# Ten modulation rows moved from the two first-block mixers to GpSimd, which makes them during the feed-forwards

## The reference, cut to what matters

```python
mod = cond @ w_ada[l] + b_ada[l]                 # cond = silu(c), one vector of 1024; w_ada[l] is 1024 x 9216
sh1, sc1, g1, sh2, sc2, g2, sh3, sc3, g3 = split(mod, 9)
y = swiglu(modulate(x, sh1, sc1), ...)           # feed-forward, inner width 2816
x = post_norm(x, y, g1, 0.5, ...)
y = token_mixer(modulate(x, sh2, sc2), w_in, w_out)
x = post_norm(x, y, g2, 1.0, ...)
y = swiglu(modulate(x, sh3, sc3), ...)           # second feed-forward
x = post_norm(x, y, g3, 0.5, ...)
```

## Time and profile before

| what | value |
|---|---|
| median of 3 runs | 2607.93 us (2603.06 to 2611.44) |
| profiled execution, device time | 2608.47 us |
| its span from first to last instruction | 2606.7 us |
| mean granted TensorE clock | 0.879 of full speed |
| busy: PE, PEld, DVE, ACT, POOL | 2114.2, 1335.6, 1023.4, 526.1, 71.9 us |
| feed-forward 1 of layer 1 | 44 to 236 us |
| first mixer | 251 to 452 us |
| feed-forward 2 of layer 1 | 464 to 656 us |
| feed-forward 1 of layer 2 | 674 to 866 us |
| second mixer | 882 to 1080 us |
| feed-forward 2 of layer 2 | 1092 to 1285 us |
| second block | 1285 us to the end |

### The profile page before, as it was taken

The page is one execution under the profiler, slowest core; times in us unless marked ns, Lnnn a source line. Parts: engine busy times, 40 slices in busy tenths (PEclk is TensorE's granted clock), DMA queues, the critical chain, the costliest instruction groups (busy, mean ns, idle before and its releaser), DMA issues.

```text
span 2606.7 us, 34365 instructions
## 1 busy us (share of the span) xinstructions
PE 2114.2 (81%) x12932; PEld 1335.6 (51%) x12932; DVE 1023.4 (39%) x1644; ACT 526.1 (20%) x858; POOL 71.9 (3%) x106
## 2 busy tenths in 40 slices
PE   6998987999899897799979676666659877777775
PEld 4996454899799545599865421211128542221111
DVE  3886134778887404588723300000022331000002
ACT  2332031443343103233312200000010110000000
POOL 1000000000000000000100000000000000000000
PEclk7998988999899898899989788888879978777777
DMA  9986742888588565488740699999995469999996
GB/s 335 321 306 218 277 139 105 301 302 304 204 297 299 191 253 194 154 301 296 274 147 18 255 405 410 410 410 410 410 389 187 164 246 410 409 410 410 409 409 247
DMA packets 289374, 758.09 MB, mean 291 GB/s; under 512 B 17616, under 2 KB 125424, under 8 KB 289184
## 3 DMA queue, kind: packets, MB, share of 16 engines
q1 hardware_dynamic: 282368, 737.34, 75.4%
q0 software_dynamic: 6688, 19.78, 2.3%
q10 hardware_dynamic: 256, 0.13, 0.0%
HBM read 756.01 MB, written 1.18 MB: 290 GB/s over the span
## 4 chain that ended last, share of the span: by engine, by line
PE 61%; DMA 24%; DVE 5%; SPq 4%; ACT 2%; issue 2%; DVEq 1%; ACTq 0%
PE psum L693 20%; DMA W<-in_w_exp_down 14%; PE psum L705 9%; DMA W<-in_w_exp_up 8%; PE psum L756 6%; PE psum L733 4%; SPq L485 4%; PE psum L1063 3%; PE psum L1039 3%; PE psum L1002 3%; PE psum L635 1%; PE psum L1027 1%; PE psum L904 1%; DMA W_mod<-in_mod_w 1%; PE psum L666 1%
## 5 line engine op out<-in xcount | busy, mean ns | idle before, releaser
L693 PE MATMUL psum<-parts 128*128 128x256 f32 x4224 | 528.8, 286 | 14.7 <-DVE parts L1490 7.4
L693 PEld LDWEIGHTS psum<-parts 128*128 128x128 f32 x4224 | 526.2, 195 | 22.4 <-issue 16.2
L1002 PE MATMUL psum<-W,scr 128*32 128x512 f32 x2048 | 316.5, 729 | 141.0 <-DMA W<-in_w_exp_up 125.9
L705 PE MATMUL psum<-parts 128*128 128x512 f32 x1056 | 257.8, 393 | 0.0
L1002 PEld LDWEIGHTS psum<-W,scr 128*32 128x32 f32 x2048 | 54.1, 118 | 378.7 <-DMA W<-in_w_exp_up 284.3
L1854 DVE TENSOR_TENSOR scr<-scr,psum 128x256 f32<-128x256 f32 x32 | 13.5, 421 | 572.5 <-ACT scr L1319 572.5
L1027 PE MATMUL psum<-W,scr 128*32 128x256 f32 x2048 | 159.0, 442 | 91.0 <-DMA W<-in_w_exp_down 75.9
L1490 DVE TENSOR_TENSOR parts<-W,parts 128x1024 fp32r<-128x1024 f32 x176 | 207.4, 1221 | 56.9 <-ACT parts L1139 56.7
L705 PEld LDWEIGHTS psum<-parts 128*128 128x128 f32 x1056 | 192.6, 188 | 45.3 <-DVE parts L1503 7.4
L1369 DVE SCALAR_TENSOR_TENSOR mod_acc<-W_mod,cond,mod_acc 128x1024 f32<-128x1024 f32 x140 | 179.8, 1285 | 27.7 <-issue 27.7
L1139 ACT ACTIVATE parts<-W 128x1024 fp32r<-128x1024 f32 x176 | 175.7, 1051 | 46.9 <-issue 46.9
(11 more groups left out here) (278 smaller groups left out, 1759.7 us busy)
## 6 DMA issues: line engine op xcount, KB each, us to landing
W<-in_w_exp_down SPq DMA_DIRECT2D x128, 1024.0 KB
W<-in_w_exp_gate SPq DMA_DIRECT2D x256, 512.0 KB, 14.9
W<-in_w_exp_up SPq DMA_DIRECT2D x256, 512.0 KB, 15.7
W_mod<-in_mod_w SPq DMA_DIRECT2D x123, 1024.0 KB, 6.5
W<-in_ffn_w_gate SPq DMA_DIRECT2D x44, 1024.0 KB, 9.5
W<-in_ffn_w_up SPq DMA_DIRECT2D x44, 1024.0 KB, 11.9
W<-in_ffn_w_down SPq DMA_DIRECT2D x44, 1024.0 KB, 9.3
W<-in_w_in SPq DMA_DIRECT2D x24, 1024.0 KB, 7.1
```

The costliest lines, as they stand in the source:

```text
L693: ins = pe.matmul(psum[:, 4 + t % 2, S * g:S * g + S], w[:, t % 2, g, kc, :], u[:, kc, :], start=(n == 0 and kc == 0), stop=(n == 2 and kc ...
L705: ins = pe.matmul(psum[:, 2 * tt + h, :], h_[:, t % 2, P * tt:P * tt + P], w[:, t % 2, 512 * h:512 * h + 512], start=(t == 0 and n == 0), ...
L1002: ins = pe.matmul(psum[32 * q:32 * q + 32, 4, :].rearrange("p (g n) -> p g n", g=2), xe_now[:, kc, :], w[:, :, q, :], start=(kc == 0), sto ...
```

## The change

The five rows of each mixer leave it. Ten rows (7, 8, 9, then 15, 16, 17, then 23, 30, 31, then 29) are made by GpSimd during the four feed-forwards: three, three, three and one. The loop passes of the feed-forwards make one row each as before, with other row numbers (`LOOP_ROW`). In a row, GpSimd loads four chunks of 1 MB through its own queue into W6 and W7 in turn, and for each of eight blocks multiplies by the column (`tensor_scalar`) and adds to a sum in `qm` (`tensor_tensor`). TensorE sums the rows of a stage over the partitions ahead of the last `down` (`side_sums`), VectorE adds the biases behind the last `hidden`, and GpSimd stores the rows (`side_store`).

```diff
+LOOP_ROW = (2, 10, 18, 24)
+SIDE_ROWS = ((7, 8, 9), (15, 16, 17), (23, 30, 31), (29,))
+side_psum = [psum[:, 7, 0:256], psum[:, 7, 256:512], psum[:, 4, 0:256]]
...
 # SyncE, loads of a mixer's weights
-                    if u >= 6:
-                        for c in (2 * (u % 2), 2 * (u % 2) + 1):
-                            mod_chunk(l * JOBS_LAYER + (FIRST_JOBS + PAIRS + (u - 6) // 2), c)
                     if u < 2:
-                        sp.wait_ge(pn_x, l * 6 + 2)
+                        sp.wait_ge(side_freed, 4 * SIDE_END[2 * l])
...
 # GpSimd
+            def side_chunk(n):
+                j, c = divmod(n, 4)
+                row = list(itertools.chain(*SIDE_ROWS))[j]
+                if n >= 2:
+                    pool.wait_ge(side_freed, n - 1)
+                pool.dma_start(part(W[:, 6 + n % 2, :], 0, 2, D), A["mod_w"][row:row + 1, 256 * c:256 * c + 256, :]
+                               .rearrange("a (k p) n -> p (a k) n", p=P)).then_inc(side_landed[n % 2], 16)
+            def side_rows(f):
+                first, end = SIDE_END[f] - len(SIDE_ROWS[f]), SIDE_END[f]
+                if f == 0:
+                    pool.wait_ge(mod_freed[1], 2 * FIRST_JOBS)
+                elif f % 2:
+                    pool.wait_ge(m_pe.s, m_pe.at("out", f // 2))
+                pool.drain()
+                side_chunk(4 * first)
+                side_chunk(4 * first + 1)
+                for j, row in enumerate(SIDE_ROWS[f]):
+                    pool.dma_start(side_bias[j:j + 97:32, :], A["mod_b"][row:row + 1, :].rearrange("a (h n) -> (a h) n", h=4)
+                                   ).then_inc(side_bias_in, 16)
+                    acc = part(qm[:, 4 * j:4 * j + 4, :].rearrange("p a b -> p (a b)"), 0, D)
+                    for c in range(4):
+                        n = 4 * (first + j) + c
+                        pool.wait_ge(side_landed[n % 2], 16 * (n // 2 + 1))
+                        for kk in range(2):
+                            w = part(W[:, 6 + n % 2, :], 0, 2, D)[:, kk, :]
+                            col = cond[:, row, 2 * c + kk:2 * c + kk + 1]
+                            if c or kk:
+                                pool.tensor_scalar(w, w, col, None, ALU.mult)
+                                pool.drain()
+                                ins = pool.tensor_tensor(acc, acc, w, ALU.add)
+                            else:
+                                ins = pool.tensor_scalar(acc, w, col, None, ALU.mult)
+                        ins.then_inc(side_freed, 1)
+                        if n + 2 < 4 * end:
+                            side_chunk(n + 2)
+            def side_store(f):
+                pool.wait_ge(side_taken, f + 1)
+                for j, row in enumerate(SIDE_ROWS[f]):
+                    pool.dma_start(mod_rows[row:row + 1, :].rearrange("a (h n) -> (a h) n", h=4), side_out[j][j:j + 97:32, :]
+                                   ).then_inc(side_stored, 16)
+                if f % 2 == 0:
+                    pool.memset(qm[:, 0:6, :], 0.0).then_inc(qm_rezeroed, 1)
+                    pool.memset(qm[:, 6:12, :], 0.0).then_inc(qm_rezeroed, 1)
...
                     if s:
                         gain(s)
                         bias(s)
-                    gate(s, 9 * l + 3 * k + 2, 16 * (9 * l + 3 * k + 3))
+                    if k != 1:
+                        side_rows(2 * l + k // 2)
+                    gate(s, 9 * l + 3 * k + 2, 9 * l + 3 * k + 3)
                     if s < 5:
                         columns(s + 1, ...)
+                    if k != 1:
+                        side_store(2 * l + k // 2)
             pool.dma_start(ctx_tok, A["ctx"].rearrange("(t p) d -> p t d", p=P)).then_inc(s_ctx, 16)
             columns(6, ...)
...
 # TensorE
+            def side_sums(f):
+                n = len(SIDE_ROWS[f])
+                pe.wait_ge(side_freed, 4 * SIDE_END[f])
+                for j in range(n):
+                    acc = part(qm[:, 4 * j:4 * j + 4, :].rearrange("p a b -> p (a b)"), 0, D)
+                    for q in range(4):
+                        ins = pe.matmul(side_psum[j][32 * q:32 * q + 32, :], K["ones"][:, 0:32], acc[:, 256 * q:256 * q + 256],
+                                        start=True, stop=True, skip_group_check=True)
+                ins.then_inc(pe_side, 1)
...
+                side_sums(2 * l + k)
                 down(TILES - 1)
...
 # TensorE, mixer: every mod_quarter and the wait for mod_taken go
-                            if kc == 3 and 1 <= g <= 3:
-                                mod_quarter(...)
...
 # VectorE, end of a feed-forward
                 hidden(TILES - 1)
+                dve.wait_ge(pe_side, f + 1)
+                dve.wait_ge(side_bias_in, 16 * SIDE_END[f])
+                for j in range(len(SIDE_ROWS[f])):
+                    ins = dve.tensor_tensor(side_out[j], side_psum[j], side_bias, add)
+                ins.then_inc(side_taken, 1)
```

More of the change, by code:

```diff
@@ L10 @@
+import itertools
 from contextlib import ExitStack
@@ L54 @@
 FIRST_JOBS = 2
-JOBS_LAYER = 3 * PAIRS
-assert FIRST_JOBS + LAYERS * JOBS_LAYER == JOBS
+JOBS_LAYER = 2 * PAIRS
+LOOP_ROW = (2, 10, 18, 24)
+SIDE_ROWS = ((7, 8, 9), (15, 16, 17), (23, 30, 31), (29,))
+SIDE_END = list(itertools.accumulate(len(rows) for rows in SIDE_ROWS))
+LOOP_ROWS = [0, 1] + [first + i for first in LOOP_ROW for i in range(PAIRS)]
+assert sorted(LOOP_ROWS + list(itertools.chain(*SIDE_ROWS))) == list(range(JOBS))
 MIX_IN_USES = IN_W * D // (P * 2048)
@@ L178, in build @@
         cond_now = sb("cond_now", [P, KC, 32])
+        side_bias = cond_now[:, :, :].rearrange("p k n -> p (k n)")
+        side_out = [mod_acc[:, 256 * j:256 * j + 256] for j in range(3)]
         cvec = sb("cvec_sb", [P, 2, 3, KC])
@@ L292, in build @@
         mod_stored = sem("mod_stored")
+        side_landed = [sem(f"side_mod_landed{s}") for s in range(2)]
+        side_bias_in = sem("side_mod_bias_landed")
+        side_freed = sem("side_mod_freed")
+        pe_side = sem("side_rows_in_psum")
+        side_taken = sem("side_rows_taken")
+        side_stored = sem("side_rows_stored")
+        qm_rezeroed = sem("qm_rezeroed")
         hi_gu = sem("gate_up_high")
@@ L377, in _, with mod_bias_row, chunk_of, mod_chunk @@
         def _(sp):
-            def mod_bias_row(job, first=False):
+            def mod_bias_row(job, row, first=False):
                 if not first:
                     sp.wait_ge(mod_taken, job)
-                sp.dma_start(mod_bias[0:97:32, :], A["mod_b"][ds(job, 1), :].rearrange("a (h n) -> (a h) n", h=4)
+                sp.dma_start(mod_bias[0:97:32, :], A["mod_b"][ds(row, 1), :].rearrange("a (h n) -> (a h) n", h=4)
                              ).then_inc(bias_landed, 16)
-            def chunk_of(job, c):
-                return A["mod_w"][ds(job, 1), 256 * c:256 * c + 256, :].rearrange("a (k p) n -> p (a k) n", p=P)
-            def mod_chunk(job, c):
+            def chunk_of(row, c):
+                return A["mod_w"][ds(row, 1), 256 * c:256 * c + 256, :].rearrange("a (k p) n -> p (a k) n", p=P)
+            def mod_chunk(job, row, c):
                 sp.wait_ge(mod_freed[c % 2], 2 * job + c // 2)
                 if c == 3:
-                    mod_bias_row(job)
-                sp.dma_start(part(W_mod[:, c % 2, :], 0, 2, D), chunk_of(job, c)).then_inc(mod_landed[c % 2], 16)
+                    mod_bias_row(job, row)
+                sp.dma_start(part(W_mod[:, c % 2, :], 0, 2, D), chunk_of(row, c)).then_inc(mod_landed[c % 2], 16)
             for job in range(FIRST_JOBS):
@@ L529, in _, with rows_stored @@
             pool.dma_start(cvec[:, 0, :, :], A["cvec"]).then_inc(s_cvec, 16)
+            def rows_stored(need):
+                pool.wait_ge(mod_stored, 16 * sum(row < need for row in LOOP_ROWS))
+                if need > min(SIDE_ROWS[0]):
+                    pool.wait_ge(side_stored, 16 * max(n + 1 for n, row in enumerate(itertools.chain(*SIDE_ROWS)) if row < need))
             def columns(s, row, need=None):
@@ L535, in columns @@
                 if need is not None:
-                    pool.wait_ge(mod_stored, need)
+                    rows_stored(need)
                     pool.wait_ge(zeroed, 3)
@@ L584, in _ @@
                         bias(s)
-                    gate(s, 9 * l + 3 * k + 2, 16 * (9 * l + 3 * k + 3))
-                    if k == 1:
-                        for j in range(1, PAIRS):
-                            set_cond(mix_job + j)
+                    if k != 1:
+                        side_rows(2 * l + k // 2)
+                    gate(s, 9 * l + 3 * k + 2, 9 * l + 3 * k + 3)
                     if s < 5:
-                        columns(s + 1, 9 * l + 3 * k + 3, 16 * (9 * l + 3 * k + 5))
-                    if k == 0:
-                        set_cond(mix_job)
+                        columns(s + 1, 9 * l + 3 * k + 3, 9 * l + 3 * k + 5)
+                    if k != 1:
+                        side_store(2 * l + k // 2)
```

(12 more changed lines are left out.)

45 lines of the change are left out of this document (16 added, 29 removed).

## The result

The changed kernel takes 2752.53 us (median of 4, 2749.9 to 2753.6), the kernel before 2608.0 in the same session: a ratio of 1.056, 95% interval 1.0538 to 1.0582. The forecast was 2734. The profiled execution spans 2748.1 us, +141.4.

| stage | us before | change | forecast |
|---|---|---|---|
| first feed-forward (three rows) | 235.7 | +49.1 | +45.8 |
| first mixer | 202.8 | -22.9 | -19.3 |
| second feed-forward (three rows) | 219.1 | +49.3 | +45.8 |
| third feed-forward (three rows) | 208.8 | +48.3 | +45.8 |
| second mixer | 200.2 | -16.2 | -18.5 |

The account below looks back on a forecast made before the run. TensorE bounds the feed-forwards, VectorE close behind with 12.6% reserve. 2608.5 + 143.0 (feed-forwards) + 8.7 (their ends) + 11.9 (behind the fourth) - 37.8 (mixers) = 2734.3, given as 2734 us, +4.8%; range 2645 to 2800.

Parts of the forecast that it names:

- Bound and mechanism: Feed-forwards: TensorE without a gap, VectorE close behind with 12.6% reserve; GpSimd instructions reading SBUF hold VectorE out.
- The signs named beforehand: Feed-forward pass from 34.78 to 45 us or more beside GpSimd, 34.78 behind it; subtraction's maximum 2 or 3 us.
- Size of the hold: Feed-forwards: a row on GpSimd holds VectorE out for 8 x 0.87 + 7 x 2.0 = 21.0 us, 0.86 of it delaying.
- A multiplication takes 1.05 us: GpSimd's one-input multiplication: 0.87 us of streaming plus 0.18 around it; part of an 11.0 us chunk, 132 us for three rows.
- The prediction's own formula: Feed-forward loss (0.86 x held - 0.126 x S) / 0.874, S the stretch: 42.9 us for three rows, 14.3 for one.
- the third rival: GpSimd late: a chunk passes 14.5 us, TensorE waits in `side_sums`; 2774 us at 20 us a chunk; chance 0.07.
- It can make up 0.126 S from its reserve: Feed-forwards: VectorE recovers 12.6% of a stretch S from its reserve, 16.6 us for three rows, 5.5 for one.
- Ends of the feed-forwards: Sums and biases before the last `down`: +2.9 us for each of three stages, +8.7 in all.
- Behind the fourth: Context load and columns for stage 6 wait behind `side_store` after the fourth feed-forward, delaying VectorE's norm: +11.9 us.
- Gain in the mixers: Projections 14.0 us shorter in each mixer, attention 5.3 and 4.5 us; 37.8 us gained in all.
- The first (DMA, 2664): Rival: VectorE hardly held, GpSimd's loads make DMA the bound in the feed-forwards, 73 us lost, 2664 us; chance 0.10.
- The second (nothing held, 2591): Rival: long instructions share the ports and loads spread evenly, so the kernel gets faster, 2591 us; chance 0.10.

Follow-up runs that it names:

- experiment 1: Changed kernel with all its loads, waits, sums and stores kept, but GpSimd's arithmetic done on 8 of 1024 columns: 2602.4 us, ratio 0.9987.
- experiment 2: Changed kernel with all of GpSimd's arithmetic, but each of its 40 block loads brings 8 of 1024 columns: 2762.7 us, ratio 1.0589.
- experiment 3: The small kernel of its own: GpSimd and VectorE instructions alone, then in pairs, without loads; VectorE's addition 1.14 us alone, 3.28 beside GpSimd's addition.
- experiment 5: Changed kernel without GpSimd's 70 additions: 2636.5 us, ratio 1.0111; without the 70 multiplications ahead of the additions: 2720.0 us, ratio 1.0434.
- experiment 4: Changed kernel with memsets replacing GpSimd's arithmetic: 6 for each multiply and add pair, 2768.6 us, ratio 1.0622; 3 for each pair, 2609.2 us, ratio 1.0014.
- experiment 6: Changed kernel with context load and columns issued ahead of the fourth feed-forward's row store: 2750.3 us; with the context's shift and scale loads ahead too: 2735.6 us.
- experiment 6's first kernel: The first repair: changed kernel with context load and next columns issued ahead of the fourth feed-forward's row store: 2750.3 us, ratio 1.0548.

## Why the prediction was right, and where it was off

**Bound and mechanism: right.** TensorE is full in a feed-forward and VectorE close behind, so what holds VectorE is paid. Experiments 1 and 2 put the loss on the arithmetic and leave nothing for the loads; 3 and 5 show the hold itself, and 4 that VectorE's subtraction is held only by an instruction that reads. The inference from one pair of late instructions held for 150. The signs named beforehand came: passes of 45.7 us and more, 34.8 behind GpSimd's end, and a maximum of 3.44 us for the subtraction.

**Size of the hold: right in sum.** Forecast 21.0 us a row, 0.86 of it felt, so 180 for ten. By experiment 5 a row holds 8 x 0.65 + 7 x 1.89 = 18.4 us as VectorE feels it, 184 for ten; its busy time grew by 1201.0 - 1023.4 = 178. With the factor of 0.86, the forecast's 0.87 and 2.0 us are 0.75 and 1.72, one somewhat above and one somewhat below. The 2.0 was a choice between 0.87 and 2.61, so its nearness is in part luck.

**"A multiplication takes 1.05 us": wrong, and it shifts the sum.** Its shortest execution is 2.85 us; only its hold is as short as I took the instruction to be. A chunk took (225.5 - 31.15) / 12 = 16.2 us and not 11.0, in part because VectorE holds GpSimd too, and in part through waits in front of the additions that the profile puts down to nothing (30.4 us from 45 to 236). So the stretch S in which VectorE can make up time was 194 us and not 132. The prediction's own formula then gives (54.1 - 0.126 x 194) / 0.874 = 33.9 us a stage (35.9 in the first, where 180 of the 194 us lie within the stage) and 11 for the one row, about 113 in place of 143. A chunk of 16.2 us also lies above the 14.5 at which the third rival begins, and experiment 4 bears that limit out. In the first stage GpSimd was in time even by the clock of the kernel before (225.5, last `down` at 234.15), since it had begun 14 us ahead of the stage. In the second it began 13.8 us into the stage and ended 205.6 us into it, where the kernel before starts its last `down` after 190.2; there only the stretched stage kept it in time. The forecast passed near a second loss without seeing it.

**"It can make up 0.126 S from its reserve": the term that was off.** A stage's loss to the holds is its change less that of experiment 1, which has the same sums: 49.1 - 3.3 = 45.8, 46.5 and 46.0 us, and 16.6 for the single row. That is 155 in all, where 143 was forecast. In the first feed-forward VectorE's busy time grew by 52.5 us, 51.4 without the three biases (54.1 forecast). So it made up 5.6 us where the forecast had 11.2, and where the formula with the true S would have 20. Its waits for ScalarE, which are the reserve, show the same. The second figure behind the bar is the idle time; first the kernel before (44 to 236 us), then the changed one (45.35 to 284.83):

```profile
L1490 DVE TENSOR_TENSOR parts<-W,parts 128x1024 fp32r<-128x1024 f32 x42 | 49.6, 1223 | 14.4 <-ACT parts L1139 14.4
L1512 DVE TENSOR_TENSOR att<-att,psum 128x256 f32<-128x256 f32 x22 | 9.2, 420 | 14.3 <-ACT att L1158 14.2
...
L1558 DVE TENSOR_TENSOR parts<-W,parts 128x1024 fp32r<-128x1024 f32 x42 | 66.6, 1625 | 13.6 <-ACT parts L1210 13.6
L1580 DVE TENSOR_TENSOR att<-att,psum 128x256 f32<-128x256 f32 x22 | 9.1, 412 | 8.7 <-ACT att L1229 8.6
```

The wait in front of the product shrank by 5.6 us; the one in front of the subtraction stayed, 56.7 us before and 58.5 after over the whole span. Why that one gives nothing back is not shown. The two mistakes, S too short and the reserve taken as wholly usable, pulled against each other, so that 143 came near 155 is in part luck.

The lower clock went beside it: TensorE's matmuls of this stage took 208.8 us and not 192.0, 1.5 of it the new sums. No run has the holds at full clock. VectorE waited only 8.6 us for the product of gate and up, which comes from TensorE through ScalarE, so as an estimate a full clock would have given back no more than about that.

**Ends of the feed-forwards: right.** +2.9 forecast; experiment 1, with the same sums and additions, shows +3.3, +2.8 and +2.3.

**Behind the fourth: right in kind, too small.** +11.9 forecast, 16.8 in experiment 1. GpSimd went on 1.4 us after TensorE began its sums, as forecast (1.2), and began its last column load 4.0 us later (3.9 forecast). But that load took 10.68 us and not 7.1, and from its landing to the norm passed 2.3 us (1422.49 to 1424.77) and not 1.3; these two make up the gap. Experiment 6 shows 17 us in this queue, and a second wait right behind, which the prediction did not see.

**Gain in the mixers: right in the projections, lucky in the rest.** 39.1 against 37.8. The projections took 85.5 us, 14.4 less, and 14.0 less in the second mixer; forecast 14.0 each. The rest of each mixer, the attention above all, gave 8.5 and 2.2 where 5.3 and 4.5 were forecast. This part differs from one execution to the next: in the profiled execution of experiment 6's first kernel, with the same code up to there, the two mixers gained 16.1 and 13.5, 29.6 in all, and the attention of the first took 86.86 us at a granted clock of 0.74 against 80.20 at 0.79.

**Rivals.** The first (DMA, 2664) fell with experiment 1: full DMA engines cost nothing there. The blocks took longer to land (a median of 9.4 us against 7.0 in the changed kernel), and the matmuls did not wait. The second (nothing held, 2591) fell with all of them; experiment 1 is what it would have given, 2602. The Trainium skill ("SBUF — State Buffer", Who interferes with whom) also puts a lock on the pair of ports for the whole instruction. For GpSimd's addition the small kernel comes near (2.1 of 2.30 us), for its multiplication it does not (0.87 of 2.82). By the letter the hold would have been 8 x 2.82 + 7 x 2.30 = 38.7 us a row, twice the 18.4 measured. For the length of an addition, the estimate of 2.25 us from the Trainium skill ("GPSIMD Engine Reference", Elementwise — side-by-side cycle accounting) agrees with 2.30.

## What to carry to other kernels

Before work goes to an idle GpSimd, ask whether VectorE has the bottleneck right behind it: each 128 x 1024 addition on GpSimd cost VectorE 1.9 us here, more than VectorE's own 1.22 for the same work, while a memset cost next to nothing. A whole row on GpSimd held VectorE for 18.4 us; VectorE makes one itself in 48.7 / 5 = 9.7 us (L1367 and L1369 in the first feed-forward of the kernel before). Look instead for a stage in which VectorE itself is idle. And when a queue gets a new wait, list everything issued behind it; the first repair here only showed the next wait in the same queue.

## What the runs showed of the hardware

- GpSimd's one-input multiplication of 128 x 1024 takes 2.82 us by a column and 2.74 by a constant, longer than its two-input addition (2.30); a copy takes 0.99 and a memset 0.90. The hold goes the other way round: 0.65 to 0.87 us for the multiplication, 1.9 to 2.1 for the addition.
- A VectorE instruction with one SBUF input is held too: its multiplication by a constant goes from 0.61 us to 0.96 beside GpSimd's multiplication and to 1.68 beside its addition, and the kernel's cast from a mean of 299 ns to 582.
- A memset on GpSimd holds that cast, though not the subtraction. With 3 memsets in each pair's place the subtractions stay at 1215/1218/1227 ns, but the cast of 128 x 256 reaches 1123 ns against 295, about one memset more, and all 88 take 36.9 us against 26.5 in experiment 1:

```profile
L1577 DVE CAST parts<-att x88: 293/295/1123, 53.7 to 1258.4; 128x256 fp32r<-128x256 f32 x88
```

- TensorE keeps its rate with the DMA engines at a share of 1.00 and 360 GB/s (experiment 1): the blocks are delayed, not the matmuls.
